# Expert choice: a threshold search by two bits a round, and lists made with 128 slot numbers

## The reference

```python
aff = jax.nn.softmax(jnp.einsum('bnd,de->ben', u, w_router_l).astype(jnp.float32), axis=1)
gate, idx = lax.top_k(aff, cap)          # cap = 256 of 2048 latent tokens, 16 of 128 context tokens
xs = jax.vmap(lambda ub, ib: ub[ib])(u, idx)
...
return jax.vmap(lambda ob, ib: jnp.zeros((N, D), ob.dtype).at[ib.reshape(-1)].add(ob.reshape(-1, D)))(out, idx)
```

## Time and profile before

| | |
|---|---|
| median of 3 runs | 3457.57 us (3457.2 to 3462.61) |
| profiled execution: time | 3458.87 us |
| profiled execution: span | 3457.2 us |
| mean granted TensorE clock | 0.902 of full speed |
| busy share of the span: PE, DVE, ACT, POOL | 85%, 50%, 35%, 22% |
| `choose`, first to last VectorE instruction | about 1911.8 to 2037.1 us |

### The profile page before, as it was taken

How to read it: one execution, slowest core, us unless ns; L and a number is a source line. 1 busy time by engine, 2 the same in 40 slices (tenths; PEclk the granted TensorE clock), 3 DMA queues, 4 the chain that set the end, 5 groups by cost and what they waited for, 6 DMA issues and landing times. The chain is left out here.

```text
span 3457.2 us, 52889 instructions
## 1 busy us (share of the span) xinstructions
PE 2947.5 (85%) x20103; PEld 2551.3 (74%) x20103; DVE 1732.9 (50%) x3539; ACT 1207.8 (35%) x2110; POOL 772.3 (22%) x1256
## 2 busy tenths in 40 slices
PE   8679999995988788787899339999999999999980
PEld 1258788884766566576687329999999999999980
DVE  2442203323544366672444575666666666666634
ACT  0441214321444433341333014444444444444422
POOL 3013400004555233461011000112211111111111
PEclk9679999996999888788899559999999999999995
DMA  7334542246777320211433235566666656556528
GB/s 269 139 123 140 180 146 83 96 155 152 178 173 170 111 71 28 88 55 45 147 111 116 104 127 168 173 186 184 185 197 184 193 171 188 179 171 193 174 71 326
DMA packets 312148, 513.98 MB, mean 149 GB/s; under 512 B 56206, under 2 KB 197558, under 8 KB 310296
## 3 DMA queue, kind: packets, MB, share of 16 engines
q1 hardware_dynamic: 283050, 410.22, 37.5%
q0 software_dynamic: 24336, 85.48, 8.7%
q10 hardware_dynamic: 4592, 16.06, 1.3%
HBM read 404.96 MB, written 122.52 MB: 153 GB/s over the span
## 5 line engine op out<-in xcount | busy, mean ns | idle before, releaser
L2499 DVE TENSOR_TENSOR ex_wlow<-ex_w,ex_whigh 128x2048 fp32r<-128x2048 f32 x192 | 440.1, 2293 | 158.8 <-ACT ex_whigh L2439 158.6
L2439 ACT ACTIVATE ex_whigh<-ex_w 128x2048 fp32r<-128x2048 f32 x192 | 366.9, 1912 | 252.9 <-DMA ex_w<-in_w_up 141.5
L2319 POOL DMA_INDIRECT ff_rows<-ex_YR,ex_sel_out x32 | 82.3, 2572 | 1081.3 <-DVE ex_YC L2491 1076.4
L2327 PE MATMUL ex_Y<-ex_hs_high,ex_whigh 128*128 128x272 f32 x1024 | 303.0, 296 | 17.1 <-DVE ex_hs_low L2515 17.1
L2327 PE MATMUL ex_G<-ex_xs_high,ex_whigh 128*128 128x272 f32 x1024 | 301.3, 294 | 2.3 <-DVE ex_xs_low L2483 2.3
L2329 PE MATMUL ex_G<-ex_xs_high,ex_wlow 128*128 128x272 f32 x1024 | 297.4, 290 | 0.0
L2329 PE MATMUL ex_Y<-ex_hs_high,ex_wlow 128*128 128x272 f32 x1024 | 297.2, 290 | 0.0
L2327 PE MATMUL ex_U<-ex_xs_high,ex_whigh 128*128 128x272 f32 x1024 | 296.9, 290 | 0.0
L2329 PE MATMUL ex_U<-ex_xs_high,ex_wlow 128*128 128x272 f32 x1024 | 296.6, 290 | 0.0
L2328 PE MATMUL ex_G<-ex_xs_low,ex_whigh 128*128 128x272 f32 x1024 | 295.6, 289 | 0.0
L2328 PE MATMUL ex_Y<-ex_hs_low,ex_whigh 128*128 128x272 f32 x1024 | 295.5, 289 | 0.0
(11 more groups left out here) (366 smaller groups left out, 7185.8 us busy)
## 6 DMA issues: line engine op xcount, KB each, us to landing
ex_w<-in_w_gate SPq DMA_DIRECT2D x64, 1024.0 KB
ex_w<-in_w_up SPq DMA_DIRECT2D x64, 1024.0 KB
ex_w<-in_w_down SPq DMA_DIRECT2D x64, 1024.0 KB
wada<-in_ada_w SPq DMA_DIRECT2D x12, 2048.0 KB, 8.2
hg_rows<-hg_pool_rows SPq DMA_DIRECT2D x68, 256.0 KB, 3.0
at_k_high<-key_parts SPq DMA_DIRECT2D x64, 256.0 KB, 4.1
hg_pool_rows<-hp_res POOLq DMA_DIRECT2D x34, 384.0 KB, 2.8
hp_w<-in_w_in SPq DMA_DIRECT2D x48, 256.0 KB
```

What stands on the lines that cost most here:

```text
L2319: pool.indirect_dma_start(ff_d, bass.IndirectOffsetOnAxis(ap=sel_out[0:n, i:i + 1], axis=0), src, None, compute_op=ALU.add).then_inc(s_sc, 16)
L2327: nc.tensor.matmul(out, wh, xh, start=start, stop=False)
L2439: nc.scalar.activation(h, v, ACT.Copy).then_inc(s_high, 1)
L2499: nc.vector.tensor_tensor(l, v, h, ALU.subtract).then_inc(s_low, 1)
```

## The change

The search takes two bits a round: three candidates (the digit 1, 2 or 3 put in) are made, all three are compared in one instruction into `trial`, TensorE counts 48 columns in place of 16, and the digit is the number of candidates that passed (`passed`, a sum over the three, a conversion to integer). So there are 15 rounds. The lists use slot numbers 0 to 127 alone: where the place is 128 or more (`upper`), 128 is taken off, and the payload goes to the second of two groups of five columns (`halves`), so that one matmul with 10 columns serves both halves.

```diff
-    BITS = 30
+    BITS, DIGIT = 30, 2
+    ROUNDS, TRIES = BITS // DIGIT, (1 << DIGIT) - 1
...
-        slot = m.sb("ch_slot", [P, CAP_LAT], BF16)
-        OH = m.sb("ch_OH", [P, 2, TILES, CAP_LAT], BF16)
+        slot = m.sb("ch_slot", [P, P], BF16)
+        OH = m.sb("ch_OH", [P, 2, TILES, P], BF16)
...
+        upper, halves = m.sb("ch_upper", [P, TILES, E_N]), m.sb("ch_halves", [P, TILES, E_N, 2, NP], BF16)
...
-                for r in range(BITS + 1):
+                for r in range(ROUNDS):
                     pe.wait_ge(s_m, r + 1)
                     for t in range(LAT_TILES):
-                        nc.tensor.matmul(pc[:, 0:E_N], one[:, :], mask[:, t, :], start=(t == 0), stop=(t == LAT_TILES - 1),
-                                         skip_group_check=True)
-                    nc.tensor.matmul(pc[:, E_N:2 * E_N], sixteen[:, :] if r < BITS else one[:, :], mask[:, CTX_TILE, :], start=True,
-                                     stop=True, skip_group_check=True).then_inc(s_cnt, 1)
+                        nc.tensor.matmul(pc[:, 0:TRIES * E_N], one[:, :], trial[:, t, :, :].rearrange("p j e -> p (j e)"), start=(t == 0),
+                                         stop=(t == LAT_TILES - 1), skip_group_check=True)
+                    nc.tensor.matmul(pc[:, TRIES * E_N:2 * TRIES * E_N], sixteen[:, :], trial[:, CTX_TILE, :, :].rearrange("p j e -> p (j e)"),
+                                     start=True, stop=True, skip_group_check=True).then_inc(s_cnt, 1)
+                pe.wait_ge(s_m, ROUNDS + 1)
+                for t in range(LAT_TILES):
+                    nc.tensor.matmul(pc[:, 0:E_N], one[:, :], mask[:, t, :], start=(t == 0), stop=(t == LAT_TILES - 1),
+                                     skip_group_check=True)
+                nc.tensor.matmul(pc[:, E_N:2 * E_N], one[:, :], mask[:, CTX_TILE, :], start=True, stop=True,
+                                 skip_group_check=True).then_inc(s_cnt, 1)
...
-                    for h in range(2):
-                        for t in range(LAT_TILES):
-                            nc.tensor.matmul(pl[e % 2][:, h * NP:(h + 1) * NP], o[:, t, h * P:(h + 1) * P], pay[:, t, e, :],
-                                             start=(t == 0), stop=(t == LAT_TILES - 1), skip_group_check=True)
+                    for t in range(LAT_TILES):
+                        nc.tensor.matmul(pl[e % 2][:, 0:2 * NP], o[:, t, :], halves[:, t, e, :, :].rearrange("p h n -> p (h n)"),
+                                         start=(t == 0), stop=(t == LAT_TILES - 1), skip_group_check=True)
...
-                for r in range(BITS):
-                    bit = 1 << (BITS - 1 - r)
-                    link(nc.vector.tensor_scalar(cand[:, :], thr[:, :], bit, None, ALU.bitwise_or))
+                def try_digits():
+                    f = cand[:, :, :].bitcast(F32)
+                    nc.vector.tensor_tensor(trial[:, 0:LAT_TILES], aff_l.unsqueeze(2).to_broadcast([P, LAT_TILES, TRIES, E_N]),
+                                            f[:, :, 0:E_N].unsqueeze(1).to_broadcast([P, LAT_TILES, TRIES, E_N]), ALU.is_ge)
+                    return nc.vector.tensor_tensor(trial[:, CTX_TILE], aff_c.unsqueeze(1).to_broadcast([P, TRIES, E_N]), f[:, :, E_N:2 * E_N], ALU.is_ge)
+
+                for r in range(ROUNDS):
+                    unit = 1 << (BITS - DIGIT * (r + 1))
+                    for j in range(TRIES):
+                        link(nc.vector.tensor_scalar(cand[:, j, :], thr[:, :], (j + 1) * unit, None, ALU.bitwise_or))
                     if r >= 1:
                         dve.wait_ge(s_cnt, r)
-                    compare(mask, cand, ALU.is_ge).then_inc(s_m, 1)
+                    try_digits().then_inc(s_m, 1)
                     dve.wait_ge(s_cnt, r + 1)
 
-                    link(nc.vector.tensor_scalar(inc[:, :], pc[:, 0:2 * E_N], CAP_LAT - 0.5, float(bit), ALU.is_ge, ALU.mult))
-                    link(nc.vector.tensor_tensor(thr[:, :], thr[:, :], inc[:, :], ALU.bitwise_or))
+                    link(nc.vector.tensor_scalar(passed[:, :, :, :], pc[:, 0:2 * TRIES * E_N].rearrange("p (g j e) -> p g j e", g=2, j=TRIES),
+                                                 CAP_LAT - 0.5, float(unit), ALU.is_ge, ALU.mult))
+                    link(nc.vector.tensor_reduce(digit[:, :, :], passed[:, :, :, :].rearrange("p g j e -> p g e j"), AX.X, ALU.add))
+                    link(nc.vector.tensor_copy(inc[:, :, :], digit[:, :, :]))
+                    link(nc.vector.tensor_tensor(thr[:, :], thr[:, :], inc[:, :, :].rearrange("p g e -> p (g e)"), ALU.bitwise_or))
...
                 link(nc.vector.tensor_scalar(place[:, :, :], place[:, :, :], -1.0, None, ALU.add))
+                link(nc.vector.tensor_scalar(upper[:, :, :], place[:, :, :], float(P) - 0.5, None, ALU.is_ge))
+                spread = upper[:, :, :].unsqueeze(3).to_broadcast([P, TILES, E_N, NP])
+                link(nc.vector.tensor_tensor(halves[:, :, :, 1, :], pay[:, :, :, :], spread, ALU.mult))
+                link(nc.vector.tensor_tensor(halves[:, :, :, 0, :], pay[:, :, :, :], halves[:, :, :, 1, :], ALU.subtract))
+                link(nc.vector.scalar_tensor_tensor(out=place[:, :, :], in0=upper[:, :, :], scalar=-float(P), in1=place[:, :, :],
+                                                    op0=ALU.mult, op1=ALU.add))
```

More of the change, by code:

```diff
@@ L2062, in choose @@
         thr = m.sb("ch_thr", [P, 2 * E_N], I32)
-        cand = m.sb("ch_cand", [P, 2 * E_N], I32)
-        inc = m.sb("ch_inc", [P, 2 * E_N], I32)
+        cand = m.sb("ch_cand", [P, TRIES, 2 * E_N], I32)
+        passed = m.sb("ch_passed", [P, 2, TRIES, E_N])
+        inc = m.sb("ch_inc", [P, 2, E_N], I32)
+        digit = m.sb("ch_digit", [P, 2, E_N])
+        trial = m.sb("ch_trial", [P, TILES, TRIES, E_N], BF16)
         one, sixteen, before = m.sb("ch_one", [P, P], BF16), m.sb("ch_16", [P, P], BF16), m.sb("ch_before", [P, P], BF16)
@@ L2093, in _ @@
                 nc.gpsimd.memset(before[:, :], 1.0).then_inc(s_k, 1)
-                nc.gpsimd.iota(slot[:, :], [[1, CAP_LAT]], base=0, channel_multiplier=0, allow_small_or_imprecise_dtypes=True)
+                nc.gpsimd.iota(slot[:, :], [[1, P]], base=0, channel_multiplier=0, allow_small_or_imprecise_dtypes=True)
                 nc.gpsimd.iota(pay[:, :, :, 0:1], [[0, ALL]], base=0, channel_multiplier=1, allow_small_or_imprecise_dtypes=True)
@@ L2104, in _ @@
                 pe.wait_ge(s_cst, 1)
-                for r in range(BITS + 1):
+                for r in range(ROUNDS):
                     pe.wait_ge(s_m, r + 1)
                     for t in range(LAT_TILES):
-                        nc.tensor.matmul(pc[:, 0:E_N], one[:, :], mask[:, t, :], start=(t == 0), stop=(t == LAT_TILES - 1),
-                                         skip_group_check=True)
-                    nc.tensor.matmul(pc[:, E_N:2 * E_N], sixteen[:, :] if r < BITS else one[:, :], mask[:, CTX_TILE, :], start=True,
-                                     stop=True, skip_group_check=True).then_inc(s_cnt, 1)
+                        nc.tensor.matmul(pc[:, 0:TRIES * E_N], one[:, :], trial[:, t, :, :].rearrange("p j e -> p (j e)"), start=(t == 0),
[8 more added lines that the diff above has]
+                                 skip_group_check=True).then_inc(s_cnt, 1)
                 for r, x in enumerate((eq, chosen)):
-                    pe.wait_ge(s_m, BITS + 2 + r)
+                    pe.wait_ge(s_m, ROUNDS + 2 + r)
                     nc.tensor.matmul(pp[:, 0:ALL], before[:, :], x[:, :, :].rearrange("p t e -> p (t e)"), start=True, stop=False,
@@ L2152, in _ @@
                 link(nc.vector.memset(thr[:, :], 0))
[L2153 to L2155 removed]
+                def try_digits():
[7 more added lines that the diff above has]
+                        link(nc.vector.tensor_scalar(cand[:, j, :], thr[:, :], (j + 1) * unit, None, ALU.bitwise_or))
                     if r >= 1:
                         dve.wait_ge(s_cnt, r)
[L2158 removed]
+                    try_digits().then_inc(s_m, 1)
                     dve.wait_ge(s_cnt, r + 1)
[L2161 to L2162 removed]
+                    link(nc.vector.tensor_scalar(passed[:, :, :, :], pc[:, 0:2 * TRIES * E_N].rearrange("p (g j e) -> p g j e", g=2, j=TRIES),
[3 more added lines that the diff above has]
+                    link(nc.vector.tensor_tensor(thr[:, :], thr[:, :], inc[:, :, :].rearrange("p g e -> p (g e)"), ALU.bitwise_or))
                 compare(mask, thr, ALU.is_gt).then_inc(s_m, 1)
                 compare(eq, thr, ALU.is_equal).then_inc(s_m, 1)
[L2165 removed]
+                dve.wait_ge(s_cnt, ROUNDS + 1)
                 nc.vector.tensor_scalar(need[:, 0:E_N], pc[:, 0:E_N], -1.0, float(CAP_LAT), ALU.mult, ALU.add)
```

## The result

The changed kernel takes 3454.05 us (median of 12 runs, 3449.05 to 3456.06); the kernel before 3460.85 (12 runs, 3457.2 to 3465.31). The ratio is 0.9976, with a 95% interval of 0.9968 to 0.9985: 8 us faster by the ratio (5 to 11), 7 by the medians. The forecast was -7.0 us and 3450.5. That number stood on the median of the first three runs, 3457.57; from the median of all twelve the same sum gives 3453.8. The prediction had given 0.48 each to "faster" and "the same", with the line between them at 6.9 us. The interval of 5 to 11 us holds that line, so the runs show a gain but decide neither for the one nor for the other.

What follows compares the result with a forecast made beforehand. Lists bound by VectorE, search by its chain of small dependent steps. 3.46 added - 1.5 (search) - 8.55 (lists) - 0.43 (last matmuls) = -7.0 us, from the median 3457.57 to 3450.5; range 3448.0 to 3454.8.

Steps and rivals of the forecast that it cites:

- The chain of the search: Search rounds on VectorE and TensorE: a two-bit round takes 3.765 us against 3.79 for two one-bit rounds, saving next to nothing.
- the sum over three: Search round, reduce of 96 elements: 0.24 dense plus 0.06 for strided reading, 0.345 us with the link.
- The first round behind GpSimd: First search round, VectorE ready under GpSimd's constants: digit 1 ends at 1917.33, where two rounds before ended at 1918.50.
- The list step: Lists, VectorE comparison with 128 slots: 0.161 to 0.163 us in place of 0.196, 8.55 us saved over 256 instructions.
- What is added ahead of the lists: VectorE between search and lists: `upper`, second update of `place` and both `halves` add 3.46 us, bounds 2.6 to 8.8.
- half of 1.04: Lower `halves`, 1360 elements bf16 throughout: half the two-source rate of 1.04 ns an element, so 0.87 us.
- The full-rate price of 1.575: Lower `halves`: alternative price of 1.575 us if bf16 operands bring no faster rate; 0.87 was taken.
- The rule on sources that aren't bf16: Added update of `place`: skill's rule halves throughput, 0.28 us longer, gain 6.8 in place of 7.1; a measured row spoke against.
- Halves at the price of single bf16 writes: Rival, both `halves` ahead of the lists: 3.95 us each, 5.3 more, 3455.8 us; chance of costly halves 0.12.
- A list step that does not shrink: Rival, lists: so short an instruction is all fixed cost, 8.55 us lost, 3459.1 us, no change; chance 0.05.
- A reduce that pays for each output: Rival, search: each of 32 outputs costs 0.06, 1.9 us a round, 29 in all, 3479 us; chance 0.04.
- A rising clock: Rival, search: larger matmuls raise TensorE's clock, columns take half, 5.3 us in all, 3445.2 us; chance 0.03.

## Why the prediction was right

The gain came as forecast and the median lies in the range, but this is in part luck: two terms were off and cancelled (0.62 us more added ahead of the lists, 0.73 more saved in the search), and the measured 3454.05 is only 0.75 under the range's upper end, because the base moved. The main mechanism held: most of the gain comes from the lists (4.9 of 7.1 us with what they need), and the rounds of the search save little.

- **The chain of the search** was read rightly: three candidates, a comparison three times as long, 48 columns and two small operations cost nearly what the second round did. The round was 3.71 and not 3.765. The one item that was off is the sum over three: 0.26 and not 0.31. I took the 0.66 ns an element that L2207 pays for reading steps of five floats for steps of sixteen, and they cost next to nothing here: 0.26 is the dense price of 96 elements. Over fourteen rounds the 0.054 a round are 0.75, the difference between 1.5 and 2.23.
- **The first round behind GpSimd** gave 1.13 of the 1.17 in the sum. That is right for the profile as it was, but not understood: the first candidate's 0.79 was itself a wait for GpSimd.
- **The list step** was right to the hundredth: 0.1625, lists -8.98, out of the two shapes in one timeline.
- **What is added ahead of the lists** was 4.08 and not 3.46. `upper`, the update of `place` (0.44) and the upper half (1.67 for 1.70) were right; the step that failed is "half of 1.04" for the lower half: 1.54 and not 0.87. The rate exists (0.869 in dense planes), but not for an output in runs of five (1.483 with dense inputs). The full-rate price of 1.575 was in the text as a bound.
- **The rule on sources that aren't bf16** (the Trainium skill, "Vector Engine (DVE) Microarchitecture Reference", section "Points that are easy to get wrong") would have made the added update of `place` 0.28 longer. It took 0.44 with two float tensors from SBUF, 1.04 ns an element on the fixed 0.157: the row decided rightly. The prediction's "6.8 in place of 7.1" for it doesn't fit its own sum of 7.0, from which 0.28 less is 6.7.
- **The rivals.** Halves at the price of single bf16 writes: no, 1.67 and 1.54 against 3.95. A list step that does not shrink: no. A reduce that pays for each output: no, 0.26 for 32 outputs. A rising clock: no, 0.50.
- **The base.** The predicted 3450.5 is 3.5 under the measured median; 3.3 of this is the kernel before, whose median moved from 3457.57 to 3460.85 with more runs. The range had no term for that.

## What to carry to other kernels

In a chain of small dependent operations, trying more candidates a round pays only if what is added per round is less than the waits saved: two bits gave 1.1 us over fourteen rounds, taking three operations off each round (two candidates and the conversion) gave 8.3, and three bits lost 10 in the rounds and 4 more in the first. Where a small instruction is mostly fixed cost, put many into one and choose the layout so that all operands are of one 16-bit type and the innermost rows are dense or at least even; check the rate in the trace, for an output in rows of five with gaps silently ran at half of it here. When an instruction's longest duration is four times its median, look at what ran on the other engines at its end before calling it a fixed cost, and measure a stage by its own span when the stages ahead vary more than the change.

## What the runs showed of the hardware that I had not expected

- A subtraction of 1360 bf16 numbers takes 0.869 us in dense operands and 1.54 (1.48 with dense inputs) with the output in runs of five at a pitch of ten; in runs of six at a pitch of twelve 1632 take 1.01.
- A one-source VectorE operation of 0.18 us from SBUF to SBUF takes up to 0.79 beside a GpSimd memset or pattern, and one of seven took 2.07 beside a row of 63 memsets of one column. A GpSimd operation moved "under cover" of a search can so lengthen it.
- The sum over rows of three at steps of 16 floats takes 0.26 for 96 elements, as if dense; over rows of seven 0.53 for 224, 0.14 above the dense price (0.157 and 1.04 ns an element).
- Loading 128x128 bf16 weights whose columns lie 32 bytes apart takes 164 ns in place of 104, one every 64 ns in place of 27.
